# Reordered loads and split waits in the close of layer 0, early weights and a moved step in the scan of layer 1

## The chip, the core and the metric

The program runs on one core of a Trainium2 chip. The metric is the device time of one execution in microseconds (us). The engines are called PE (matmul, with PEld for its weight loads), DVE (vector), ACT (activations), POOL (GpSimd) and SP (the queue from which nearly all transfers of this kernel are issued). A matmul of float32 shows as two records.

## What is computed

The reference is two blocks of a network on 1024 tokens of width 1024. The first block has two layers; the second one (a hybrid mixer and 16 experts) is untouched here. What matters is the end of layer 0 and the start of layer 1:

```python
def _mixer_ab(...):                       # layer 0
    oa = dilated_attention(...)           # three dilations, merged by a softmax of their log sums
    ob = bidirectional_gated_scan(...)    # forward + backward, 4 heads of 256
    ob = _head_rmsnorm(ob, norm_gain)
    y = jnp.concatenate([oa, ob], axis=-1) * jax.nn.silu(gate)
    return jnp.einsum('bsf,fd->bsd', y, w_out)

def _mixer_c(...):                        # layer 1
    proj = jnp.einsum('bsd,df->bsf', h, w_in)
    q, f_f, f_b, i, gate = _split(proj, (C_WIDTH,) * 5)        # 12 heads of 128
    f = lb + (1.0 - lb) * jax.nn.sigmoid(z)                    # forward and backward
    o = bidirectional_gated_scan(silu(q) * s, 1 - f, log(f), ..., i)
    ...
x = _layer_norm(DEEPNORM_ALPHA * x + y, ln_gain[layer], ln_bias[layer])
```

## The kernel before

The program is a chain of stages. Each stage allocates its buffers and semaphores, runs one instruction stream per engine, and ends in a barrier of all engines. Two stages are touched.

**The close of layer 0** (`close_layer`, tag `end`, from 1061 to 1304 us) works on 8 tiles of 128 tokens. Below, n is the tile; the first two and the last two are written out, the four between run in a loop. For a tile

- SP's `load` fetches `of` and `ob` (the scan forward and backward, 512 KB each), `gt` (the gate, 768 KB) and `parts` (the three attention parts, 792 KB), in this order, after `y_done` of the tile before. All four raise the one semaphore `loaded[b]`, on which DVE, ACT and POOL wait for all of them. `load_x` fetches the residual `xt`.
- `front`: DVE merges the parts (L1475 to L1501) into `y[:, 0:A]`, with one Exp by ACT (L1380) in the middle. POOL adds `of + ob` (L1352). ACT takes Silu of the gate (L1381), squares the sum (L1386) and takes the root (L1389). DVE scales by root and gain into `y[:, A:W]` (L1510, `normed`), POOL multiplies all of `y` by the gate (L1355, `y_done`).
- PE turns `y` (L1430), ACT copies it (L1397), PE multiplies by the weights `w` (L1448, 48 records, banks `ps_z[0]` then `ps_z[1]`, `z_made`), then turns the tile before (L1438).
- DVE adds the residual and normalizes (L1526 to L1537, `centred`), POOL multiplies by gain and adds the bias (L1364, L1366, `x_done`), SP stores.

On each engine `front` of tile n + 1 stands ahead of the rest of tile n. At the start SP issues `load(0, 0)`, the vectors `gains`, `lng` and `lnb` (512 KB each, on one semaphore `vec_loaded`, for which DVE waits ahead of everything), `w` (6144 KB, one transfer), `load_x(0, 0)`, and then `load(0, 1)`, which waits for `y_done`.

**The scan of layer 1** (`projected_scan`, tag `hgrn`, 1304 to 2304 us) computes the projections as it goes. A unit of columns (`f`, `q`, `vg`, ...) takes seven sub-products of a Strassen scheme, called fills: SNAP1, PLAIN, SNAP21, SNAP22, JOIN22, JOIN21, LAST. The weights come through a ring of three slots. Four banks `ps_w` take the fills in turn; SNAP21 accumulates in the bank of SNAP1, after ACT has copied it (`moved`). DVE makes four sums of activations (L441 to L446, `x_made`) and POOL four sums of weights per unit (L758, L760, L765, L772, `s_made`); SNAP21 needs the second of DVE and the third of POOL. ACT's first instruction is the Sigmoid of the bounds (L1200), which waits for `diff_done`; DVE raises that after its four sums (L1088). ACT's copies of fills (`take`) stand behind it.

Four units are computed ahead of the first step. Then come 96 steps, 8 for each of 12 heads; step p of head h is g = 8h + p. In a step PE does `front` of step g + 1 (scores L899; transposes L907, which wait for `out_moved` to reach g, that is for `move_out(g - 1)`), `update(g)` (L916), `output(g)` (L929, L932) and the fills planned for it. DVE and ACT prepare head h + 1 along the way by `prepare(h + 1, p)`: DVE's `sums` at p = 2 and 3 (L988 to L999, `rel_done`), its `spans_of` at p = 3 and 4 (L1007 to L1017, `points_done`), behind each other in its queue. ACT's own order in a step is

```python
                if g:
                    move_out(g - 1)
                    takes(of_step[g - 1])
                if (g + 1) % TILES < CARRIED and g + 1 < STEPS:
                    move_keys((g + 1) // TILES, (g + 1) % TILES)
                if h + 1 < heads:
                    prepare(h + 1, p)
```

and its `exps` at p = 3 and 4 wait for `rel_done`, compute `qd` and `kd` (L1171, L1172), wait for `points_done`, and compute `end_decay` and `pair_decay` (L1174, L1175). Users of the decays are DVE's `scale_keys` from p = 6 on and POOL's `scale_queries` of the next head.

## Time and profile before

| what | us |
|---|---|
| time, median of 3 runs | 4135.04 (4132.1 to 4139.99) |
| time of the profiled execution | 4133.34 |
| its span, first to last instruction | 4131.6 |
| close of layer 0: stage, PE busy | 243.00, 193.73 |
| scan, ahead of the steps (1304 to 1433): PE busy | 129.00, 121.74 |
| scan, 96 steps (1433 to 2304): PE busy | 871.00, 817.96 |
| whole span: PE, DVE, ACT, POOL busy | 3580.3, 1779.0, 1076.0, 1171.5 |

The profile is that of one execution. The time of that execution is 1.7 us above its span. A row of the timeline gives start, duration, engine, line, operation and shapes, a count if rows were merged, and in brackets how long the engine had sat idle before it and what ended that. In a row of waits stand the total, the number of times and the longest.

### The profile page before, as it was taken

The numbers are of one execution on the slowest core, as the hardware profiler recorded it, in microseconds if no ns is written. First come the engines' busy times: TensorE is split into PE (matmuls) and PEld (weight loads), VectorE is DVE, ScalarE is ACT, GpSimd is POOL, SyncE is SP. The second block draws the span as 40 slices with busy tenths as digits, with TensorE's granted clock in tenths as the row PEclk, the third lists the DMA queues.
The fourth block names the chain that finished last, engine by engine and source line by source line (L and its number), as shares of the span: only waits on it lengthen the run. The fifth ranks groups of instructions, "written<-read, shape, count | busy, mean of one in ns | idle before, by whom it ended". The sixth has DMA issues, their size and how long they took to land. (4 is left out here: it accounts for less than half of the span.)

```text
span 4131.6 us, 46995 instructions
## 1 busy us (share of the span) xinstructions
PE 3580.3 (87%) x16369; PEld 2331.9 (56%) x16369; DVE 1779.0 (43%) x4038; ACT 1076.0 (26%) x2201; POOL 1171.5 (28%) x940
## 2 busy tenths in 40 slices
PE   8889998888697999999988598998975776949996
PEld 4645676667443675675646445655655775424442
DVE  0025552433353266566575353243477577240001
ACT  1023433432232233233233252221212212211111
POOL 0000000333243355456555354000303445211110
PEclk9999999899898999999999797999997888969998
DMA  3264532231432111121111533113224721446996
GB/s 114 77 169 146 164 113 85 70 99 47 191 143 87 53 54 45 53 61 48 56 48 39 221 133 108 38 44 117 92 93 131 255 98 58 159 171 234 315 325 229
DMA packets 408272, 494.01 MB, mean 120 GB/s; under 512 B 70498, under 2 KB 314490, under 8 KB 408051
## 3 DMA queue, kind: packets, MB, share of 16 engines
q1 hardware_dynamic: 379431, 457.42, 33.3%
q0 software_dynamic: 4608, 16.78, 1.6%
q10 hardware_dynamic: 24012, 16.97, 1.3%
q8 instruction: 126, 2.06, 0.2%
q14 instruction: 95, 0.78, 0.1%
HBM read 362.32 MB, written 128.77 MB: 119 GB/s over the span
## 5 line engine op out<-in xcount | busy, mean ns | idle before, releaser
L817 POOL TENSOR_TENSOR hgrn_queries<-hgrn_qd,hgrn_pair_decay 128x640 f32<-128x640 f32 x192 | 274.7, 1450 | 324.3 <-PE hgrn_ps_a L932 290.1
L867 PE MATMUL hgrn_ps_w<-xT,hgrn_ring 128*128 128x512 f32 x432 | 195.6, 599 | 8.9 <-DMA hgrn_ring<-in_w_in_c_dram 8.9
L395 PE MATMUL gla_bg_ps<-gla_bg_w,xT 128*128 128x256 f32 x768 | 196.6, 403 | 4.0 <-DMA gla_bg_w<-in_w_in_ab_dram 4.0
L395 PEld LDWEIGHTS gla_bg_ps<-gla_bg_w,xT 128*128 128x128 f32 x768 | 151.8, 203 | 37.7 <-issue 10.6
L1448 PE MATMUL end_ps_z<-end_w,end_yT 128*128 128x512 f32 x384 | 169.7, 602 | 1.6 <-ACT end_yT L1397 1.6
L2535 PE MATMUL end_ps_z<-end_w,end_yT 128*128 128x512 f32 x384 | 167.0, 595 | 0.8 <-ACT end_yT L2463 0.8
L391 PE MATMUL att_bg_ps<-xT,att_bg_w 128*128 128x512 f32 (+1 forms) x288 | 136.9, 615 | 13.3 <-POOL att_ident L1755 13.3
L867 PEld LDWEIGHTS hgrn_ps_w<-xT,hgrn_ring 128*128 128x128 f32 x432 | 81.4, 193 | 101.2 <-issue 91.6
L45 POOL MEMSET gla_ident<- 128x128 f32 x1 | 0.2, 205 | 484.5 <-POOLq L34 484.5
L1037 DVE TENSOR_TENSOR hgrn_k_end<-hgrn_kd,hgrn_end_decay 128x128 f32<-128x128 f32 x168 | 126.7, 793 | 8.9 <-issue 2.2
L872 PE MATMUL hgrn_ps_w<-hgrn_ring,xT 128*128 128x256 f32 x576 | 130.3, 382 | 0.0
L867 PE MATMUL hgrn_ps_w<-hgrn_xs,hgrn_wsum 128*128 128x512 f32 x288 | 128.2, 592 | 0.0
L2048 POOL TENSOR_TENSOR gla_queries<-gla_qd,gla_pair_decay 128x640 f32<-128x640 f32 x64 | 89.9, 1423 | 131.1 <-PE gla_ps_o L2111 91.5
L2891 PE MATMUL in_ps<-hT_cols,in_w 128*128 128x512 f32 x288 | 126.2, 592 | 0.0
L1448 PEld LDWEIGHTS end_ps_z<-end_w,end_yT 128*128 128x128 f32 x384 | 73.7, 194 | 92.6 <-issue 89.8
L4751 PE MATMUL exp_ps_d<-expw_wd,exp_hidT 128*128 128x512 f32 x256 | 114.1, 599 | 11.0 <-ACT exp_hidT L4698 11.0
L395 PE MATMUL att_bg_ps<-att_bg_w,xT 128*128 128x256 f32 x512 | 123.4, 387 | 0.0
L2535 PEld LDWEIGHTS end_ps_z<-end_w,end_yT 128*128 128x128 f32 x384 | 72.7, 191 | 89.6 <-issue 88.3
L1874 ACT ACTIVATE att_p_sb<-att_s_sb,att_shift 128x256 f32<-128x256 f32 (+1 forms) x192 | 88.8, 464 | 121.3 <-DVE att_shift L1833 121.2
L227 PE MATMUL in_ps<-xT,in_wbuf 128*128 128x512 f32 x256 | 112.8, 604 | 8.6 <-PEq L34 8.6
L872 PEld LDWEIGHTS hgrn_ps_w<-hgrn_ring,xT 128*128 128x128 f32 x576 | 109.3, 193 | 14.6 <-issue 0.5
L4733 PE MATMUL exp_ps_g<-expw_wg,exp_xT 128*128 128x512 f32 x256 | 115.6, 605 | 0.7 <-ACT exp_xT L4687 0.7
(643 smaller groups left out, 7663.9 us busy)
## 6 DMA issues: line engine op xcount, KB each, us to landing
expw_wg<-in_exp_w_gate_dram SPq DMA_DIRECT2D x16, 2048.0 KB, 9.5
expw_wu<-in_exp_w_up_dram SPq DMA_DIRECT2D x16, 2048.0 KB, 16.3
expw_wd<-in_exp_w_down_dram SPq DMA_DIRECT2D x16, 2048.0 KB, 21.8
att_w_ada<-in_ada_w_dram SPq DMA_DIRECT2D x24, 1024.0 KB, 6.3
hgrn_ring<-in_w_in_c_dram SPq DMA_DIRECT2D x18, 1024.0 KB, 5.3
end_gt<-gate_l SPq DMA_DIRECT2D x16, 768.0 KB, 7.9
hgrn_ring<-in_w_in_c_dram SPq DMA_DIRECT2D x24, 512.0 KB, 5.5
hgrn_o<-hgrn_o_stage SPq DMA_DIRECT2D x192, 64.0 KB, 1.6
```

Source lines behind the costliest of these rows:

```text
L227: last = pe.matmul(bank[0:job.rows, 0:job.span], w[:, k, b * job.rows:(b + 1) * job.rows], job.acts[:, k, s:s + job.span], start=(k == 0), ...
L391: last = pe.matmul(bank[0:job.rows, 0:job.span], w[:, k, b * job.rows:(b + 1) * job.rows], job.acts[:, k, s:s + job.span], start=(k == 0), ...
L395: last = pe.matmul(bank[0:job.rows, q * job.width:(q + 1) * job.width], job.acts[:, k, t * P:t * P + job.rows], w[:, k, 0:job.width], star ...
L817: pool.tensor_tensor(queries[:, d, s, :].rearrange("p (b a c) -> p b a c", b=POINTS, a=PC), q, f, ALU.mult).then_inc(queries_done, 1)
L867: last = pe.matmul(bank[:, :], a[:, k, :], x(k), start=(fresh and k == 0), stop=(k == HK - 1), skip_group_check=True)
L872: last = pe.matmul(bank[:, q * 2 * P:(q + 1) * 2 * P], x(k)[:, t * P:(t + 1) * P], a[:, k, :], start=(fresh and q == 0 and k == 0), stop=( ...
L1037: dve.tensor_tensor(k_end[:, d, p % 2, :].rearrange("p (a c) -> p a c", c=CH), kd[:, b, d, t * P:(t + 1) * P].rearrange("p (a c) -> p a c" ...
L1448: made = pe.matmul(ps_z[h][:, :], yT[:, k, :], w[:, k, h * BANK:(h + 1) * BANK], start=(k == 0), stop=(k == NB - 1))
L2535: made = pe.matmul(ps_z[h][:, :], yT[:, k, :], w[:, k, halves[h]], start=(k == 0), stop=(k == NB - 1))
L2891: last = pe.matmul(ps[(3 * n + part) % 2][:, 0:span], w[u % 3][:, k, b * P:(b + 1) * P], acts, start=(k == 0), stop=(k == KB - 1))
L4733: last = pe.matmul(ps_g[:, :], xT[:, b, k, :], wg[:, b, k, :], start=(k == 0), stop=(k == KB - 1))
L4751: last = pe.matmul(ps_d[g][:, :], hidT[:, j, :], wd[:, b, j, g * BANK:(g + 1) * BANK], start=(j == 0), stop=(j == FB - 1))
```

## The change

- `load` issues `parts` first, on a semaphore of its own (`parts_loaded`), then `of` and `ob` on `loaded`, then `gt` on `gt_loaded`. DVE waits for the parts alone, POOL for `of` and `ob`, ACT's Silu for the gate.
- DVE's wait for all three vectors goes. It waits for `gains` where L1510 first uses them; POOL waits for the other two ahead of its first slot.
- `w` comes in two halves of 512 columns, each with a semaphore; PE waits for a half ahead of the 24 records that use it, in the first tile.
- POOL multiplies `y` by the gate in two pieces: `y[:, 0:A]` once the merge is done, `y[:, A:W]` after `normed`.
- The ring of the scan is allocated around both stages. SP issues its first three blocks (3 MB in four transfers) in the last slot of the close, after the store of tile 6 and ahead of the wait for tile 7, and waits for them at the end of the stage. In the scan, waits for these blocks go.
- ACT's two decay factors leave `exps` and become `decays(h, d)`, both called at p = 5. Ahead of the steps the order stays.

```diff
+def scan_weights(sp, ring, w, C, loaded):
+    rows = w.rearrange("(k p) n -> p k n", p=P)
+    for slot, at, col, width in ((0, 0, C, P), (0, P, 2 * C, P), (1, 0, 0, 2 * P), (2, 0, 3 * C, 2 * P)):
+        sp.dma_start(ring[:, slot, :, at:at + width], rows[:, :, col:col + width]).then_inc(loaded, 16)
+    return 64
...
-        counts[slot_of(b)] += 16 * len(cols)
+        counts[slot_of(b)] += 16 * len(cols) if b >= RING else 0
...
-            load(0)
             sp.dma_start(bound_in[:, :, :], bounds.rearrange("(h p) c -> p h c", p=P)).then_inc(bounds_loaded, 16)
-            for b in range(1, RING):
-                load(b)
...
+            def decays(h, d):
                 act.wait_ge(points_done, 2 * h + d + 1)
                 act.activation(end_decay[:, h % 2, d, :], ends[:, d, :], ACT.Exp)
                 act.activation(pair_decay[:, h % 2, d, :], pairs[:, d, :], ACT.Exp).then_inc(decay_done, 1)
...
                 elif p in (3, 4):
                     exps(h, p - 3)
+                elif p == 5:
+                    decays(h, 0)
+                    decays(h, 1)
...
                 wait(sp, y_done, 2 * i + b)
+                if attn is not None:
+                    sp.dma_start(parts[:, :, :], attn[:, rows(i, b), :].rearrange("a p n -> p a n")).then_inc(parts_loaded[b], 16)
                 sp.dma_start(of[:, b, :], o[0][rows(i, b), :]).then_inc(loaded[b], 16)
                 sp.dma_start(ob[:, :], o[1][rows(i, b), :]).then_inc(loaded[b], 16)
-                sp.dma_start(gt[:, b, :], gate[rows(i, b), :]).then_inc(loaded[b], 16)
-                if attn is not None:
-                    sp.dma_start(parts[:, :, :], attn[:, rows(i, b), :].rearrange("a p n -> p a n")).then_inc(loaded[b], 16)
+                sp.dma_start(gt[:, b, :], gate[rows(i, b), :]).then_inc(gt_loaded[b], 16)
...
-            sp.dma_start(w[:, :, :], w_out.rearrange("(k p) n -> p k n", p=P)).then_inc(w_loaded, 16)
+            for h in range(2):
+                half = slice(h * BANK, (h + 1) * BANK)
+                sp.dma_start(w[:, :, half], w_out.rearrange("(k p) n -> p k n", p=P)[:, :, half]).then_inc(w_loaded[h], 16)
...
+                if last:
+                    ahead_due.append(ahead(sp, ahead_loaded))
                 sp.wait_ge(x_done, 2 * i + b + 1)
...
-                pool.wait_ge(loaded[b], 16 * LOADS * i + 16 * LOADS)
+                pool.wait_ge(loaded[b], 32 * i + 32)
                 pool.tensor_tensor(of[:, b, :], of[:, b, :], ob[:, :], ALU.add).then_inc(summed, 1)
+                pool.wait_ge(gated, n + 1)
+                if A:
+                    pool.wait_ge(merged_done, n + 1)
+                    pool.tensor_tensor(y[:, 0:A], y[:, 0:A], gt[:, b, 0:A], ALU.mult)
                 pool.wait_ge(normed, n + 1)
-                pool.wait_ge(gated, n + 1)
-                pool.tensor_tensor(y[:, :], y[:, :], gt[:, b, :], ALU.mult).then_inc(y_done, 1)
+                pool.tensor_tensor(y[:, A:W], y[:, A:W], gt[:, b, A:W], ALU.mult).then_inc(y_done, 1)
...
                 for h in range(2):
+                    if first:
+                        pe.wait_ge(w_loaded[h], 16)
...
-            dve.wait_ge(vec_loaded, 48)
             front(0, 0)
```

## Rows read from the trace of the kernel before

**Rows 1.** Busy time by engine in the scan's steps.

```profile
1433.00:2304.00 871.00, 817.96 (x4726) 546.53 (x4724) 534.00 (x1079) 277.42 (x466) 465.96 (x288) 0.97 0.17 52
```

**Rows 2.** Timeline of the close, tile 0.

```profile
1074.52 0.17 DVE L1475 TENSOR_TENSOR end_top<-end_parts 128x8 f32<-128x8 f32 x1 [23.11 <-DMA end_lnb<-in_ln_bias_dram]
...
1083.61 3.42 POOL L1355 TENSOR_TENSOR end_y<-end_y,end_gt 128x1536 f32<-128x1536 f32 x1 [11.25 <-DVE end_y L1510]
...
1090.71 0.50 PEld L1448 LDWEIGHTS end_ps_z<-end_w,end_yT 128*128 128x128 f32 x2 [1.15 <-DMA end_w<-in_w_out_ab_dram]
1090.74 23.62 PE L1448 MATMUL end_ps_z<-end_w,end_yT 128*128 128x512 f32 x48 [0.78 <-ACT end_yT L1397]
```

**Rows 3.** Transfers of 1061 to 1090 us: total; size and us to landing.

```profile
DMA packets 2923, 10.95 MB, mean 378 GB/s; under 512 B 128, under 2 KB 128, under 8 KB 2922
...
end_w<-in_w_out_ab_dram SPq DMA_DIRECT2D x1, 6144.0 KB, 25.9
```

**Rows 4.** Transfers of the close's inner tiles, 1120 to 1240 us.

```profile
end_parts<-attn SPq DMA_DIRECT2D x4, 792.0 KB, 8.3
...
end_of<-gla_o SPq DMA_DIRECT2D x4, 512.0 KB, 3.6
```

**Rows 5.** PE's timeline in the close, tiles 4 and 7.

```profile
1190.66 1.52 PE L1430 MATMUL end_ps_y<-end_ident,end_y 128*128 128x128 f32 x12 [1.53 <-POOL end_y L1355]
...
1192.98 20.87 PE L1448 MATMUL end_ps_z<-end_w,end_yT 128*128 128x512 f32 x48
...
1266.28 2.16 PE L1430 MATMUL end_ps_y<-end_ident,end_y 128*128 128x128 f32 x12 [3.11 <-POOL end_y L1355]
```

**Rows 6.** DVE and POOL in the close around tiles 4 and 5.

```profile
1200.57 2.34 POOL L1352 TENSOR_TENSOR end_of<-end_of,end_ob 128x1024 f32<-128x1024 f32 x1 [1.46 <-DMA end_parts<-attn]
...
1211.77 3.42 POOL L1355 TENSOR_TENSOR end_y<-end_y,end_gt 128x1536 f32<-128x1536 f32 x1 [8.87 <-DVE end_y L1510]
1219.11 2.35 POOL L1364 TENSOR_TENSOR end_xn<-end_z,end_lng 128x1024 f32<-128x1024 f32 x1 [3.91 <-DVE end_z L1537]
...
1200.64 2.29 DVE L1475 TENSOR_TENSOR end_top<-end_parts 128x8 f32<-128x8 f32 x1 [6.45 <-DMA end_parts<-attn]
```

**Rows 7.** Timeline of the scan's entry, by engine.

```profile
1311.26 8.88 PE L867 MATMUL hgrn_ps_w<-xT,hgrn_ring 128*128 128x512 f32 x16 [8.94 <-DMA hgrn_ring<-in_w_in_c_dram]
1319.98 7.03 PE L867 MATMUL hgrn_ps_w<-hgrn_xs,hgrn_wsum 128*128 128x512 f32 x16
...
1311.02 2.29 DVE L446 TENSOR_TENSOR hgrn_xs<-xT,hgrn_xs 128x2048 f32<-128x2048 f32 x1
...
1314.50 0.21 ACT L1200 ACTIVATE hgrn_low<-hgrn_room 128x12 f32<-128x12 f32 x1 [9.22 <-DVE hgrn_room L1088]
...
1311.29 3.15 POOL L758 TENSOR_TENSOR hgrn_wsum<-hgrn_ring 128x512 f32<-128x512 f32 x1 [10.98 <-DMA hgrn_ring<-in_w_in_c_dram]
```

**Rows 8.** Waits of PE and ACT in the scan's steps, 1433 to 2303 us.

```profile
ACT hgrn_end_decay L1174 <- DVE hgrn_pairs L1017: 55.0, 13, 5.8
...
PE hgrn_ps_a L907 <- ACT hgrn_o_stage L1186: 27.1, 8, 5.8
...
PE hgrn_ps_w L867 <- DVE hgrn_q_act L966: 13.3, 5, 2.7
```

**Rows 9.** Timeline of steps 3 and 4 of head 2, ACT and PE.

```profile
1639.75 1.04 ACT L1172 ACTIVATE hgrn_kd<-hgrn_cum 128x1024 f32<-128x1024 f32 x1
1644.73 0.24 ACT L1174 ACTIVATE hgrn_end_decay<-hgrn_ends 128x40 f32<-128x40 f32 x1 [3.94 <-DVE hgrn_pairs L1017]
...
1634.05 0.44 PE L907 MATMUL hgrn_ps_a<-hgrn_ident,hgrn_k_end 128*128 128x128 f32 x2
...
1635.67 7.07 PE L872 MATMUL hgrn_ps_w<-hgrn_wsum,hgrn_xs 128*128 128x256 f32 x32
...
1645.61 0.41 PE L907 MATMUL hgrn_ps_a<-hgrn_ident,hgrn_k_end 128*128 128x128 f32 x2 [2.44 <-ACT hgrn_o_stage L1186]
...
1648.37 4.09 PE L872 MATMUL hgrn_ps_w<-hgrn_ring,xT 128*128 128x256 f32 x16
```

More of the change, by code:

```diff
@@ L446, in strassen_sums, with projected_scan @@
     dve.tensor_tensor(xs[:, 2, :, :], x(1, 0), xs[:, 1, :, :], ALU.subtract).then_inc(made, 1)
-def projected_scan(nc, tag, heads, xT, w, bounds, out, gate_out, spill, q_scale):
+def scan_weights(sp, ring, w, C, loaded):
[3 more added lines that the diff above has]
+    return 64
+def projected_scan(nc, tag, heads, xT, w, ring, bounds, out, gate_out, spill, q_scale):
     PC = P // CH
@@ L581, in projected_scan @@
         pbank = lambda n: ctx.enter_context(nc.psum_tensor(f"{tag}_{n}", [P, BANK], F32))
-        ring = sb("ring", [P, RING, KB, 2 * P])
         xs = sb("xs", [P, 3, HK, BANK])
@@ L754, in sums_early @@
                 for n in range(1 if narrow(units[u][0][0]) else 2):
-                    pool.wait_ge(w_loaded[slot_of(b + n)], loads_by[b + n])
+                    wait(pool, w_loaded[slot_of(b + n)], loads_by[b + n])
                 if u:
@@ L851, in fill @@
                     for m in range(1 if narrow(kind) else 2):
-                        pe.wait_ge(w_loaded[slot_of(b + m)], loads_by[b + m])
+                        wait(pe, w_loaded[slot_of(b + m)], loads_by[b + m])
                 e = before_on[f]
@@ L1205, in _ @@
             exps(0, 0)
+            decays(0, 0)
             takes(lead[18:25])
             exps(0, 1)
+            decays(0, 1)
             takes(lead[25:])
@@ L1228, in row_to_all, with close_layer @@
     return vector.rearrange("(a n) -> a n", a=1).to_broadcast([P, n])
-def close_layer(nc, tag, x, x_next, xT_next, o, gate, gain, w_out, ln_gain, ln_bias, V, alpha, attn=None, attn_heads=0):
+def close_layer(nc, tag, x, x_next, xT_next, o, gate, gain, w_out, ln_gain, ln_bias, V, alpha, ahead, attn=None, attn_heads=0):
     WO = o[0].shape[1]
@@ L1272, in close_layer @@
         ps_x = [pbank(f"ps_x{n}") for n in range(2)]
-        vec_loaded, w_loaded, consts = sem("vec_loaded"), sem("w_loaded"), sem("consts")
-        LOADS = 3 if attn is None else 4
+        vec_loaded, w_loaded, consts = sem("vec_loaded"), [sem("w_loaded0"), sem("w_loaded1")], sem("consts")
         loaded = [sem("loaded0"), sem("loaded1")]
+        gt_loaded, parts_loaded = [sem("gt_loaded0"), sem("gt_loaded1")], [sem("parts_loaded0"), sem("parts_loaded1")]
         x_loaded = [sem("x_loaded0"), sem("x_loaded1")]
+        gains_loaded, merged_done = sem("gains_loaded"), sem("merged_done")
         summed, squared, gated = sem("summed"), sem("squared"), sem("gated")
@@ L1323, in _ @@
             load(0, 0)
-            for dst, src in ((gains, gain), (lng, ln_gain), (lnb, ln_bias)):
+            sp.dma_start(gains[:, :], row_to_all(gain, WO)).then_inc(gains_loaded, 16)
+            for dst, src in ((lng, ln_gain), (lnb, ln_bias)):
                 sp.dma_start(dst[:, :], row_to_all(src, dst.shape[1])).then_inc(vec_loaded, 16)
-            sp.dma_start(w[:, :, :], w_out.rearrange("(k p) n -> p k n", p=P)).then_inc(w_loaded, 16)
+            for h in range(2):
+                half = slice(h * BANK, (h + 1) * BANK)
+                sp.dma_start(w[:, :, half], w_out.rearrange("(k p) n -> p k n", p=P)[:, :, half]).then_inc(w_loaded[h], 16)
             load_x(0, 0)
@@ L1500, in front @@
                         if a:
-                            dve.tensor_tensor(y[:, 0:A], y[:, 0:A], merged[:, :], ALU.add)
+                            last = dve.tensor_tensor(y[:, 0:A], y[:, 0:A], merged[:, :], ALU.add)
                             dve.drain()
+                    last.then_inc(merged_done, 1)
                 dve.wait_ge(squared, n + 1)
@@ L1507, in front @@
                 dve.drain()
+                if isinstance(i, int) and n == 0:
+                    dve.wait_ge(gains_loaded, 16)
                 for h in range(H):
@@ L4806, in network @@
             ])
-        close_layer(nc, "end0", x[0], x1, xT, gla_o, gate_l0, gla_norm[0], w_out_ab[0], ln_gain[0], ln_bias[0],
-                    B // 4, alpha, attn=attn, attn_heads=AH)
-        gate_l1 = dram("gate_l1", SEQ, C)
-        hgrn_o = [dram(f"hgrn_o{d}", SEQ, C) for d in range(2)]
-        projected_scan(nc, "hgrn", C // P, xT, w_in_c[0], hgrn_bounds, hgrn_o, gate_l1, dram("v_spill", SEQ, 2 * P), scale)
+        with nc.sbuf_tensor("hgrn_ring", [P, 3, KB, 2 * P], F32) as ring:
+            close_layer(nc, "end0", x[0], x1, xT, gla_o, gate_l0, gla_norm[0], w_out_ab[0], ln_gain[0], ln_bias[0],
+                        B // 4, alpha, lambda sp, loaded: scan_weights(sp, ring, w_in_c[0], C, loaded), attn=attn, attn_heads=AH)
+            gate_l1 = dram("gate_l1", SEQ, C)
+            hgrn_o = [dram(f"hgrn_o{d}", SEQ, C) for d in range(2)]
+            projected_scan(nc, "hgrn", C // P, xT, w_in_c[0], ring, hgrn_bounds, hgrn_o, gate_l1, dram("v_spill", SEQ, 2 * P), scale)
     poolT = dram("poolT", 2 * P, SEQ)
```

10 lines of the change are left out of this document (6 added, 4 removed).

## The prediction, on record before the change was run

> **What bounds the kernel now.** I read the windows by stage first. In the steps of the scan PE is busy 818 of 871 us [rows 1], so nearly every us there is PE's, and only what holds PE up can be won. Then the timeline of the close, for what each tile waits for; then the transfers; then the waits of PE in the scan, and around one of them the timelines of ACT and PE. The stages are divided by barriers, so what a stage gains the end of the program gains, unless a later stage waits for something else.
>
> The first tile of the close is a chain. DVE starts at 1074.5 because of the last of three vectors, not because of its data; POOL finishes `y` at 1087.0, and PE multiplies from 1090.7 [rows 2]. The queue moves 10.95 MB in this time at 378 GB/s, and `w` lands 25.9 us after its issue at 1064.4, so at 1090.3 [rows 3]: chain and weights end together. In the inner tiles PE waits some 1.5 us per tile for POOL's `y`, and 3.1 us at tile 7 [rows 5]; such a tile takes 1215.33 - 1190.66 = 24.7 us, and 23.2 without its wait. At the scan's entry PE waits for the ring until 1311.3 [rows 7]. In the steps PE waits 8 times, 27.1 us, for ACT's `move_out`, which stands behind ACT's own wait for `spans_of` [rows 8].
>
> **Part 1, the close.** *Start.* With parts first and no vector ahead of DVE, the merge starts when the parts land. `of`, as first transfer, lands after 3.6 us; parts, as fourth, after 8.3 [rows 4]. Scaled by size, parts as first take some 4.5 us, so they land at 1065.5, and DVE starts 9 us earlier. But the same bytes come before the gate: the four transfers (2.6 MB) have landed by about 1070, one table load and Silu, squares, root and scaling (8.3 us from there) follow, then the last two thirds of POOL's 3.42 us [rows 2]: `y` is done at about 1080.7 instead of 1087.0. The multiplication starts 3.4 us later as before, at 1084.1, 6.6 us earlier. It needs only the first half of `w`. Of the 10.5 MB up to the end of `w` the first half needs 7.4; with `w` whole at 1090.3 and 3.15 MB at some 390 GB/s [rows 3] it is there at about 1082.3. The second half is needed 12 us after the start; covered. If rows of 2 KB run a tenth slower than those of 4 KB, `w` is whole 1.6 us later, and the first half comes at 1083; still covered, but the next tile's loads queue behind it.
>
> *Tile 1.* Its loads queue behind `w` as before, until about 1091.7, so its gate lands no earlier than before (about 1099); only the order gains: `y` at about 1109.7 instead of 1114.6. PE, ready at 1107.7, waits 2 us. The multiplication starts at 1112.5 instead of 1117.0: 4.5 us are left of the 6.6.
>
> *Inner tiles.* Let T be `z_made`. The multiplication began at 1192.98 and took 20.87 us [rows 5], so T = 1213.85, and DVE has centred the tile when POOL's L1364 starts, at T + 5.3 [rows 6]. Until now DVE then waited for data; now the parts are there, and it starts at once. From L1475 to L1355 the front took 1211.77 - 1200.64 = 11.1 us, of which 2.1 in a lock: a DVE operation on 128x8 elements took 2.29 us beside POOL's L1352 [rows 6]. The new start puts DVE under three POOL operations (L1364, L1366, L1352), not one, so two more locks of 2.35: T + 5.3 + 11.1 + 4.7 = T + 21.1, then POOL's second piece (2.3) and about 0.9 in which the first piece holds DVE: T + 24.3. PE alone gives 23.2 per tile, and `y` of tile n + 2 hangs on T of tile n: two tiles in 23.2 + 24.3 = 47.5, or 23.2 to 23.75 a tile. I take 23.4, against 24.7: 1.3 for each of tiles 3 to 6. Tile 2 started its multiplication 27.4 us after tile 1, because of 2.6 us of wait and a low clock; it gains 4. Tile 7 gains 2.5 of 3.1 and the lower clock behind. Sum: 4.5 + 4 + 4 x 1.2 + 2 = 15. Bounds: 8 if the locks eat all gain of the inner tiles, 18 if none costs.
>
> Here the Trainium skill says the same of the cause ("SBUF — State Buffer", Who interferes with whom, and SBUF: two separate sides): DVE with two SBUF inputs and a GpSimd operation exclude each other for the whole instruction. By that rule every POOL operation that now lies over the merge costs its full length; without the lock the loop would be PE's alone, 23.2 a tile, and this part 18. The row agrees: 2.29 us for 8 elements.
>
> **Part 2, the ring at the scan's entry.** The four transfers are issued after the store of tile 6 and land within some 10 us, 20 us ahead of the barrier; they delay only the issue of the last store's wait, covered. PE can start at the entry, R = 1304, not 1311.3. What is late next: SNAP21, at R + 16.0 before [rows 7]. It needs ACT's copy of SNAP1, and ACT's queue begins with L1200, which waits for DVE's four sums. Before, these ran alone (L446, the last, from 1311.02 to 1313.31), L1200 ran at R + 10.5, and POOL's first sum took 3.15 us, because it waited for the end of L446; its own time is what is left, 1.1 to 1.27 [rows 7]. Now POOL's four sums start with DVE's four. Taking turns they end at R + 9.3 + 4 x 1.2 = R + 14.1; L1200, the copy (0.6) and three handoffs end at R + 15.2. PE gains 0.8 us. But its idle time now lies behind its first 16 records, not ahead: after 8.94 us idle they took 8.88 us instead of 7.03 [rows 7], and after 6.3 us idle I charge the same 1.85 again. Sum: 1.0 us lost. Bounds: 1.9 lost (clock alone) to 4.4 won (no lock, SNAP21 at R + 11.6, clock kept). The records on either side decide for the lock, so I take 1 lost.
>
> **Part 3, the decays.** The step of [rows 9]: ACT finishes `kd` at 1640.8 and could do `move_out` then, but waits for `spans_of` until 1644.7; PE's transposes, due at 1643.2, start at 1645.6. From transposes to fill PE took 2.76 us, against 1.62 in the step before, and 16 records of the fill 3.92 against 3.45: the clock had dropped. So 2.4 + 1.1 + 0.5 = 4.0 us a time. With the decays at p = 5, `move_out` is done at 1641.2, before PE is due. This pattern comes in heads 0, 2, 4, 6: 16 us. The other four waits (17.2 of the 27.1 us) are in heads 8 and 10, which have few fills. There PE, once free at p = 3, meets ACT held at p = 4 by the wait that stays, for `sums` (L999), which itself sits under POOL's operations. I follow both: about 3 us each are left. In the odd heads PE waits for DVE's join (13.3 us, 5 times [rows 8]); the change does not touch it. The decays cost 0.24 and 0.32 us, at p = 5 in odd heads with one more table load; ACT is busy 277 of 871 us [rows 1], and `move_out(5)` behind them has a whole step before PE needs it. Sum 22; bounds 14 (if half of the waits come back as waits for L999) and 27 (the waits in full, nothing behind).
>
> **Sum**, against the profiled execution's 4133.3: -15 + 1 - 22 = -36, so 4097.3; the median of the runs stood 1.7 above that execution: 4099.
>
> **Rivals.**
> - *The decay waits move* to L999 in all heads, or to `pick`, which stands behind `spans_of` in DVE's queue. For: DVE has no gap in this stretch. Against: in heads 0 to 6 L999 is done before PE is due. Then part 3 gives 10 to 12: 4110. Chance 0.2.
> - *The lock eats the close's loop*: tiles stay at 24.7, part 1 gives 8: 4106. Chance 0.12.
> - *The ring gives its whole wait*: no turns taken, SNAP21 at R + 11.6, clock kept: part 2 wins 4.4: 4094, and to 4091 with part 1 at its bound. Speaks against it the 3.15 us row. Chance 0.1.
> - *The change does not do what it says*: waits as before: 4133. Chance 0.03.
> - *Slower*: the decays at p = 5 come late for their users at p = 6 and the next head's queries. Then each of 11 heads waits; with the gains of the close it decides from (36 + 8) / 11 = 4 us per head on. Against: a step is about 9 us long and the decays need 1.1. Price at 5 us per head: 4144. Chance 0.05.
> - The forecast itself: 0.5.
>
> 0.2% (8 us) is what a measurement of this kernel can tell from no change. Faster by more: 0.9; within: 0.06; slower: 0.04. The bounds of the parts together are -53 and -20; all at one end is unlikely, and the rivals reach 4110: range 4084 to 4115.
>
> **What would show it.** Right: DVE's first merge near 1065.5; `y` of tile 0 near 1080.7; multiplications starting 23.2 to 23.8 apart; DVE's 128x8 operations of 2 us under L1364 and L1366; PE's first record in the scan at the entry, then a gap of 5 to 7 us ahead of the second group of 16; no waits of L907 for L1186 in heads 0 to 6, some of 3 to 4 us in heads 8 and 10. Wrong: a loop at 24.7; SNAP21 11 to 12 us behind the entry; transposes waiting for ACT in every even head.

## The result

The changed kernel takes 4102.4 us (median of 4 runs, 4101.2 to 4110.4), the kernel before 4134.1 (4 runs): a ratio of 0.9924, 95% interval 0.9911 to 0.9936, so 31.7 us less. The forecast was 4099. The profiled execution has a span of 4101.0 us at a mean clock of 0.924.

The windows first: the steps of the scan in the changed kernel, the stretch that answers to [rows 1].

```profile
1416.00:2267.00 851.00, 810.48 (x4727) 540.63 (x4725) 539.37 (x1079) 283.81 (x471) 469.11 (x288) 0.98 0.18 53
```

The same number of matmuls to one record (4727, 4726 before), in 851 us instead of 871. PE is idle for 41 us instead of 53, and has 7.5 us less of busy time, which is the clock (the granted clock is 0.98, not 0.97). Now the timeline of the close, tile 0, against [rows 2]:

```profile
1065.61 0.17 DVE L1498 TENSOR_TENSOR end_top<-end_parts 128x8 f32<-128x8 f32 x1 [14.13 <-DMA end_parts<-attn]
1066.76 1.28 ACT L1404 ACT_TABLE_LOAD   x1
1070.07 1.48 ACT L1404 ACTIVATE end_gt<-end_gt 128x1536 f32<-128x1536 f32 x1 [2.03 <-DMA end_gt<-gate_l]
...
1077.13 2.34 POOL L1377 TENSOR_TENSOR end_y<-end_y,end_gt 128x1024 f32<-128x1024 f32 x1 [1.55 <-DVE end_y L1536]
...
1083.37 20.84 PE L1473 MATMUL end_ps_z<-end_w,end_yT 128*128 128x512 f32 x48 [0.96 <-DMA end_w<-in_w_out_ab_dram]
1109.79 2.82 PE L1453 MATMUL end_ps_y<-end_ident,end_y 128*128 128x128 f32 x12 [5.58 <-POOL end_y L1377]
```

The reader is to see DVE's start 8.9 us earlier, `y` at 1079.5 (1080.7 was forecast), the first half of `w` landing just as PE wants it, and 5.6 us of PE's wait for tile 1's `y`. DVE and POOL around tile 5, against [rows 6]:

```profile
1187.69 1.45 DVE L1498 TENSOR_TENSOR end_top<-end_parts 128x8 f32<-128x8 f32 x1 [1.00 <-DMA end_parts<-attn]
...
1189.45 4.48 DVE L1503 TENSOR_TENSOR end_lift<-end_parts,end_top 128x8 f32<-128x8 f32 x3
...
1191.56 2.35 POOL L1371 TENSOR_TENSOR end_of<-end_of,end_ob 128x1024 f32<-128x1024 f32 x1
...
1202.62 2.34 POOL L1377 TENSOR_TENSOR end_y<-end_y,end_gt 128x1024 f32<-128x1024 f32 x1 [1.55 <-DVE end_y L1536]
...
1205.10 1.52 PE L1453 MATMUL end_ps_y<-end_ident,end_y 128*128 128x128 f32 x12
1206.46 1.04 PE L1461 MATMUL end_ps_x<-end_ident,end_xn 128*128 128x128 f32 x8
1207.41 20.87 PE L1473 MATMUL end_ps_z<-end_w,end_yT 128*128 128x512 f32 x48
```

`y` is done at 1204.96, and PE turns it at 1205.10 with no wait. The eight multiplications start at 1083.37, 1113.30, 1138.03, 1161.35, 1184.32, 1207.41, 1230.43 and 1253.40, the inner ones 23.0 to 23.3 apart. The scan's entry, against [rows 7], PE and then ACT:

```profile
1287.41 8.87 PE L871 MATMUL hgrn_ps_w<-xT,hgrn_ring 128*128 128x512 f32 x16 [1.77 <-PEq L34]
1301.57 8.63 PE L871 MATMUL hgrn_ps_w<-hgrn_xs,hgrn_wsum 128*128 128x512 f32 x16 [5.29 <-ACT hgrn_sig L1153]
...
1300.82 0.21 ACT L1209 ACTIVATE hgrn_low<-hgrn_room 128x12 f32<-128x12 f32 x1 [12.17 <-DVE hgrn_room L1092]
1300.94 0.58 ACT L1153 ACTIVATE hgrn_sig<-hgrn_ps_w 128x512 f32<-128x512 f32 x1
```

PE starts at the entry, then stands for 5.3 us, and its second group is 14.2 us behind the entry where it was 15.9 (14.8 and 15.1 in two more profiles with the old entry, before_again and only_decays). The waits of PE in the steps, against [rows 8]:

```profile
PE hgrn_ps_s L903 <- DVE hgrn_state L1071: 16.4, 3, 10.7
PE hgrn_ps_w L871 <- DVE hgrn_q_act L970: 13.2, 5, 2.7
PE hgrn_ps_s L903 <- POOL hgrn_queries L821: 5.5, 3, 2.7
```

The 27.1 us for ACT's `move_out` are gone but for 0.3. The second row was there before. The first is all but new (0.6 us before): 10.7 us of it are one wait in head 8. In head 2, 0.8 us of wait for DVE's `k_end` took the place of the old one.

### The profile page after: what moved, and what is told of

Read it like the earlier page. It is cut to its first block and busy times, and to the rows that moved or that the text cites. A ratio compares the mean times of both kernels' runs of the same rounds, so it can differ in the third digit from the quotient of the medians.

```text
span 4101.0 us, 47003 instructions
## 1 busy us (share of the span) xinstructions
PE 3579.0 (87%) x16369; PEld 2330.3 (57%) x16369; DVE 1812.7 (44%) x4038; ACT 1081.5 (26%) x2206; POOL 1183.6 (29%) x948
## 5 line engine op out<-in xcount | busy, mean ns | idle before, releaser
L876 PE MATMUL hgrn_ps_w<-hgrn_ring,xT 128*128 128x256 f32 x576 | 128.8, 380 | 0.0
L876 PEld LDWEIGHTS hgrn_ps_w<-hgrn_ring,xT 128*128 128x128 f32 x576 | 108.0, 191 | 14.2 <-issue 0.5
## 6 DMA issues: line engine op xcount, KB each, us to landing
expw_wg<-in_exp_w_gate_dram SPq DMA_DIRECT2D x16, 2048.0 KB, 10.3
```

What stands on the lines that cost most here:

```text
L876: last = pe.matmul(bank[:, q * 2 * P:(q + 1) * 2 * P], x(k)[:, t * P:(t + 1) * P], a[:, k, :], start=(fresh and q == 0 and k == 0), stop=( ...
```

## Where the time went, stage by stage

Four marks cut each profile: the scan's entry (DVE's first sum), the start of PE's third group of 16 fill records there, PE's first record of the next layer's close, and PE's first record in the experts' stage. The columns are the entry's time from the span's start, and then the three stretches, in us. All kernels of the study are in it, those of the next section too.

```
kernel               entry     to group 3   to next close   to experts
before               1304.04   22.81        1002.05         1393.87
before_again         1302.42   21.69        1001.74         1393.79
only_decays          1301.54   21.94         981.92         1400.75
after                1287.41   22.63         981.76         1400.84
after_again          1286.29   22.66         981.67         1403.45
no_ring              1284.95   22.20         984.24         1399.01
w_whole              1288.17   23.71         982.76         1401.42
parts_last           1285.55   24.07         983.22         1409.85
one_piece            1287.95   24.04         983.29         1403.43
copy_first           1286.93   15.65         984.70         1398.44
no_ring_copy_first   1284.28   22.19         982.26         1400.43
spans_later          1287.48   22.83         965.18         1401.25
both                 1284.69   15.67         965.12         1400.00
after_delayed        1287.20   22.64        1015.68         1400.35
```

The first profile against the first: 16.6 us won up to the entry, 0.2 at the entry, 20.3 in the scan's steps, and 7.0 lost in stages that the change does not touch; 30.1, of a difference of spans of 30.6. The same kernel repeats to 0.1 or 0.3 us in the steps, but the old close ended at 1301.5, 1302.4 and 1304.0 in three profiles, so the first one flatters the change: against their mean 15.8 were won up to the entry (two profiles of the changed kernel: 1286.9), and the entry lost 0.5 (22.65 against 22.15). That 0.5 lies within the spread of the old entry, 21.7 to 22.8, so whether the entry lost or won a little is not shown.

The column of the entry also holds the stages ahead of the close, which no edit touches: the close issues its first load between 1058.6 and 1061.9 us in the fourteen profiles. Measured from that issue, the close took 243.0, 240.5 and 240.3 us before (before, before_again, only_decays), and 226.3 and 226.2 in the changed kernel: 15.0 us won against the mean. In w_whole it took 227.6, in parts_last and one_piece 226.9. One profile with the changed close stands apart, no_ring_copy_first with 222.6; its second multiplication started 1.9 us and its third 3.6 us sooner behind the first load than in the changed kernel.

The profiles overstate what was given back behind. The two profiled executions of the kernel before took 4133.3 and 4128.3 us, both below the median of its 34 runs in the whole study (4135.3). By the medians 31.7 us were won.

## The experiments

**only_decays.** The kernel before with the decays in a step of their own, nothing else.

```diff
                 act.activation(kd[:, h % 2, d, :], ...)
+
+            def decays(h, d):
                 act.wait_ge(points_done, 2 * h + d + 1)
...
+                elif p == 5:
+                    decays(h, 0)
+                    decays(h, 1)
```

> The kernel before with one part of the change alone: the decays at p = 5. Theory (the parts add up): in the steps of the scan it gains what the changed kernel gained there, 20.3 us between the third group of the entry and the first multiplication of the next close; the eight waits of L907 for ACT's move_out are gone, in heads 8 and 10 PE waits for DVE's state instead, 10 and 5 us. Close and entry as before. Time: 20 us less at the start of the next close, and 15 to 20 less at the end, by whether the stages behind give something back. Rival (part of the 20 us came from the close, by a better clock or another phase at the start): under 15 us in the steps.

4117.7 us, 0.9966 of the kernel before (0.9954 to 0.9978), 14 us less by the ratio, 16 by the medians of the two. The steps took 981.92 us: 20.0 less, as in the changed kernel. The parts add up, and some of the 20 us are missing at the end here too: 7 by the last column (1400.75), 4 to 6 by the times. Its waits in the steps:

```profile
PE hgrn_ps_s L899 <- DVE hgrn_state L1067: 16.8, 2, 11.3
PE hgrn_ps_w L867 <- DVE hgrn_q_act L966: 13.3, 5, 2.7
```

So the new wait comes with the decays, not with the close or the ring.

**no_ring.** The changed kernel, its ring loaded at the scan's entry as before.

```diff
-                if last:
-                    ahead_due.append(ahead(sp, ahead_loaded))
...
+            load(0)
             sp.dma_start(bound_in[:, :, :], ...)
+            for b in range(1, RING):
+                load(b)
```

> The changed kernel without its ring ahead: the four transfers at the scan's entry, as before. Theory (PE's second group is set by ACT's queue, whose first entry waits for DVE's four sums): PE starts 7.3 us behind the entry, the second group of 16 at about 16.0 us, the third at 22.9; the changed kernel had the third at 22.65, so this one is within 1 us of it. Rival (the early ring is worth its wait): 5 to 7 us slower than the changed kernel.

4101.7 us (0.9928, 0.9915 to 0.9942), against 4102.4: the early ring is worth nothing. The second group followed the first without a gap and at full clock (granted clock 1.00, 0.82 in the changed kernel's second group), and the third started 22.20 us behind the entry:

```profile
1291.20 9.24 PE L874 MATMUL hgrn_ps_w<-xT,hgrn_ring 128*128 128x512 f32 x16 [8.03 <-DMA hgrn_ring<-in_w_in_c_dram]
1300.28 7.03 PE L874 MATMUL hgrn_ps_w<-hgrn_xs,hgrn_wsum 128*128 128x512 f32 x16
```

**copy_first.** The changed kernel; ACT copies the first group's bank before its Sigmoid of the bounds.

```diff
+            lead = of_step[-1]
+            takes(lead[0:1])
             act.wait_ge(diff_done, 1)
             act.activation(low[:, :], room[:, :], ACT.Sigmoid).then_inc(low_done, 1)
-            lead = of_step[-1]
-            takes(lead[0:7])
+            takes(lead[1:7])
```

> The changed kernel with one step of ACT's queue put ahead: the copy of the first group's bank (L1153) before the Sigmoid of the bounds (L1209), which waits for DVE's four sums. Theory (the order in ACT's queue holds SNAP21): the copy runs at about 5.5 us behind the entry, POOL's third sum is done at 7.8, so the second group follows the first at 8.9 without a gap, at full clock (7.0 us, not 8.6), and the third starts at 16 to 17 instead of 22.65: 5.5 to 7 us less at the first step. Rival A (the turns that DVE and POOL take set it): second group at 13 to 14, gain under 1 us. Rival B (the next wait, DVE's first join behind the same Sigmoid, takes it over): 1 to 4 us of gain are left.

4093.2 us (0.9901, 0.9886 to 0.9917), 9 us less than the changed kernel, by intervals that just overlap; the stages tell more. The entry, POOL, ACT and PE:

```profile
1291.61 3.11 POOL L769 TENSOR_TENSOR hgrn_wsum<-hgrn_ring 128x512 f32<-128x512 f32 x1 [0.16 <-issue]
1292.48 0.60 ACT L1153 ACTIVATE hgrn_sig<-hgrn_ps_w 128x512 f32<-128x512 f32 x1 [6.69 <-PE hgrn_ps_w L871]
...
1295.71 7.03 PE L871 MATMUL hgrn_ps_w<-hgrn_xs,hgrn_wsum 128*128 128x512 f32 x16
...
1302.58 3.60 PE L871 MATMUL hgrn_ps_w<-xT,hgrn_ring 128*128 128x512 f32 x8
```

The copy ran 5.6 us behind the entry, the second group 8.8 behind it, and the third 15.65: 7.0 us sooner. DVE and POOL still took turns (3.11 us for a sum that alone takes 1.26), and it did not matter. The order of ACT's queue was what held SNAP21; at the entry both rivals fell. Not all of the 7.0 reached the next close: the steps took 984.70 us, 2.9 more than in the changed kernel. One fill, behind PE's wait for DVE's join in head 3, took 6.78 us here and 3.70 there. In both (below), where that wait is short, nothing is lost.

**no_ring_copy_first.** Both edits above.

> The kernel with the copy ahead, without the early ring. Theory (the ring ahead is worth its time only when ACT's queue does not hold SNAP21): PE starts 6 us behind the entry, its second group follows without a gap at about 15, the third at 22: 5.5 us later than with the early ring and about as without either edit, so 5 to 6 us slower than the kernel with both. Rival (the ring ahead is worth nothing in any order): same as that kernel within 1 us.

4104.3 us (0.9926, 0.9912 to 0.9939), 10 to 11 us slower than with the early ring, again by intervals that overlap a little. The third group started at 22.19, to 0.01 where no_ring had it: without the early ring the copy's place is worth nothing, without the copy's place the ring is worth nothing, together they are worth 7 at this point.

**spans_later.** The changed kernel; DVE prepares the points of the first direction one step later.

```diff
                 elif p == 3:
-                    spans_of(h, 0)
                     sums(h, 1)
                 elif p == 4:
+                    spans_of(h, 0)
                     spans_of(h, 1)
```

> The changed kernel with DVE's spans_of for the first direction moved from p = 3 to p = 4, beside that for the second. Theory (in heads 8 and 10 PE waits for the state, L1071, which stands in DVE's queue behind spans_of and sums, 11.2 us at one stretch, 5 of them spans_of): the waits of 10.7 and 5.1 us shrink to 4 to 6 and 0 to 2, and since p = 4 then holds both spans_of, up to half comes back there: 3 to 8 us less in the steps of the scan, all in these two heads. Rival (DVE is the bound in these two heads whatever the order): the sum of the waits stays at 16, the time too.

4083.2 us (0.9878, 0.9863 to 0.9893), 19 us less than the changed kernel, 16.6 of them in the steps: my theory was wrong in size and in place. The waits in the steps:

```profile
PE hgrn_ps_s L903 <- POOL hgrn_queries L821: 13.9, 4, 8.4
PE hgrn_ps_s L903 <- DVE hgrn_state L1071: 6.6, 4, 2.8
PE hgrn_ps_w L871 <- DVE hgrn_q_act L970: 3.6, 5, 0.7
```

In heads 8 and 10 the wait for the state only changed its name: 16.4 + 5.5 us for state and queries became 6.6 + 13.9. There the rival was right, DVE and POOL are the bound. The gain came from the odd heads' wait for DVE's join, which fell from 2.65 to 0.71 us, five times (9.7 us):

```profile
1538.51 3.70 PE L871 MATMUL hgrn_ps_w<-xT,hgrn_wsum 128*128 128x512 f32 x8 [0.71 <-DVE hgrn_q_act L970]
```

Behind the short wait the fill takes 3.70 us (granted clock 1.00). Behind the long one it had taken 5.4 in four of the five places (granted clock 0.68), and that is nearly all of the rest. From one such wait to the next, two heads on, it is 153.4 us; in the changed kernel it was 155.3 to 157.9. DVE's queue in p = 3 had held the join all along.

**both.** copy_first and spans_later together.

> The two edits that gained, together in the changed kernel: ACT's copy of the first group's bank ahead of its Sigmoid of the bounds, and spans_of of the first direction at p = 4. Theory (they act in different stretches and add up): the third group of the entry 7.0 us earlier, the steps from there to the next close 16.6 us shorter, so about 23 to 26 us less than the changed kernel: 4076 to 4080. Rival (what is won is given back in the stages behind): under 17 us.

4076.0 us (0.9859, 0.9843 to 0.9875), 26 us less than the changed kernel and 58 to 61 less than the one before. The table has 15.67 at the entry and 965.12 in the steps: each edit's full gain.

**w_whole.** The changed kernel with `w` in one transfer.

```diff
-            for h in range(2):
-                half = slice(h * BANK, (h + 1) * BANK)
-                sp.dma_start(w[:, :, half], ...).then_inc(w_loaded[h], 16)
+            sp.dma_start(w[:, :, :], ...).then_inc(w_loaded[0], 16)
```

> The changed kernel with w in one transfer again, PE waiting for all of it. In the changed kernel the first multiplication started at 1083.37, when w's first half had landed, ended about 1104, and PE then waited 5.6 us for y of tile 1. Theory (tile 1's y sets the loop's start, whose data lie behind w in the queue; the halves win time that tile 1 gives back): the first multiplication starts 6 to 7 us later, at about 1090, PE's wait for y of tile 1 goes to nothing, the second one starts at 1113.5 to 1115, so 0 to 2 us are lost. Rival (the first tile's 7 us count in full): 6 us lost. The prediction's own bookkeeping (1112.5 against 1117.0) had the first half's 6.6 us worth 4.5.

4105.6 us (0.9922, 0.9909 to 0.9936), the same as the changed kernel. The first multiplication started 6.5 us later, the second 2.5 and the third 0.8:

```profile
1089.90 23.83 PE L1471 MATMUL end_ps_z<-end_w,end_yT 128*128 128x512 f32 x48 [8.11 <-DMA end_w<-in_w_out_ab_dram]
1113.57 1.47 PE L1451 MATMUL end_ps_y<-end_ident,end_y 128*128 128x128 f32 x12
1115.83 20.87 PE L1471 MATMUL end_ps_z<-end_w,end_yT 128*128 128x512 f32 x48 [0.79 <-ACT end_yT L1418]
```

In the changed kernel PE waited 5.6 us for tile 1's `y`, and its second multiplication took 22.63 us (granted clock 0.92); here there is no such wait, and it takes 20.87 (1.00). The close is 1.3 us longer (227.6): the halves are worth about 1 us.

**parts_last.** The changed kernel, the attention's parts fourth again in each tile's loads.

```diff
-                if attn is not None:
-                    sp.dma_start(parts[:, :, :], ...).then_inc(parts_loaded[b], 16)
                 sp.dma_start(of[:, b, :], ...)
                 sp.dma_start(ob[:, :], ...)
                 sp.dma_start(gt[:, b, :], ...)
+                if attn is not None:
+                    sp.dma_start(parts[:, :, :], ...).then_inc(parts_loaded[b], 16)
```

> The changed kernel with the attention's parts fourth again in each tile's loads, behind both halves and the gate. Theory (the order of the loads is what shortens the inner tiles: DVE no longer waits for data): DVE's merge starts 3 to 5 us later in each tile, y comes that much later, the inner tiles go back from 23.2 to 24.5 to 25 us, and the close is 8 to 12 us longer than in the changed kernel. Rival (the pieces of POOL's multiplication and the late waits carry the gain, the order does not): within 3 us of the changed kernel.

The theory fell. From the third on the multiplications are 23.0 and 23.5 to 24.0 apart in turns (117.1 us from the third to the last, 115.4 in the changed kernel), and the close as a whole takes 226.9 us, 0.6 more than in the changed kernel. Tile 5 again, DVE and POOL:

```profile
1188.58 2.34 POOL L1371 TENSOR_TENSOR end_of<-end_of,end_ob 128x1024 f32<-128x1024 f32 x1
1189.31 1.64 DVE L1498 TENSOR_TENSOR end_top<-end_parts 128x8 f32<-128x8 f32 x1 [5.59 <-DMA end_parts<-attn]
1191.27 0.32 DVE L1503 TENSOR_TENSOR end_lift<-end_parts,end_top 128x8 f32<-128x8 f32 x3
...
1200.26 2.34 POOL L1377 TENSOR_TENSOR end_y<-end_y,end_gt 128x1024 f32<-128x1024 f32 x1 [1.55 <-DVE end_y L1536]
```

DVE starts 4.6 us later behind the end of the multiplication two tiles back (10.1 us, not 5.5), but POOL's three operations are all but over by then: L1503 takes 0.32 us and not 4.48. `y` comes 23.35 us behind that end, against 22.7. The whole program took 4109.9 us (0.9934, 0.992 to 0.9949), 4 us more than the changed kernel by the ratio and 7.5 by the medians. The table has them in its last column, not in the close. Most of them can be placed: the stage of the second block with the tag `gdns` took 136.5 us here and 129.6 in the changed kernel. DVE there, in parts_last and then in the changed kernel, and POOL in parts_last:

```profile
3245.50 6.74 DVE L4089 TENSOR_TENSOR gdns_resid<-gdns_vb,gdns_rest 128x384 f32<-128x384 f32 x1
...
3242.36 2.02 DVE L4089 TENSOR_TENSOR gdns_resid<-gdns_vb,gdns_rest 128x384 f32<-128x384 f32 x2
...
3245.50 1.61 POOL L3978 TENSOR_TENSOR gdns_kw<-gdn_k_n,to_end 128x384 f32<-128x384 f32 x2
3247.07 1.61 POOL L3997 TENSOR_TENSOR gdns_kept<-gdns_state,gdns_col 128x384 f32<-128x384 f32 x2
```

One DVE operation took 6.74 us, where two take 2.02. It started together with a row of eight POOL operations, one behind the other, and ended 0.4 us after the last of them; PE's next product stood for 7.5 us. In none of the other thirteen profiles does a DVE operation of this stage take over 2.2 us. Whether the other executions of parts_last have it too is not known.

**one_piece.** The changed kernel, POOL's multiplication by the gate undivided.

```diff
                 pool.wait_ge(gated, n + 1)
-                if A:
-                    pool.wait_ge(merged_done, n + 1)
-                    pool.tensor_tensor(y[:, 0:A], y[:, 0:A], gt[:, b, 0:A], ALU.mult)
                 pool.wait_ge(normed, n + 1)
-                pool.tensor_tensor(y[:, A:W], y[:, A:W], gt[:, b, A:W], ALU.mult).then_inc(y_done, 1)
+                pool.tensor_tensor(y[:, :], y[:, :], gt[:, b, :], ALU.mult).then_inc(y_done, 1)
```

> The changed kernel with POOL's multiplication by the gate undivided again (one operation of 3.4 us behind DVE's last, not 1.2 under DVE and 2.3 behind it). Theory (y of tile n + 2 hangs on the multiplication of tile n, as the prediction had it, and in the changed kernel y comes just as PE is free, at 23.0 to 23.3 a tile): y comes 1.1 us later, two tiles take 23.2 + 24.3 instead of 23.2 + 23.2, so 0.5 us a tile and 2 to 4 us in the close. Rival (DVE's own work without POOL's first piece beside it ends earlier, 0.9 us, and PE's slack covers the rest): under 1 us.

4102.8 us (0.9918, 0.9903 to 0.9934). In the close: `y` 23.4 us behind the end of the multiplication two tiles back, PE waits 0.8, 0.56 and 0.31 us for it in every second tile, and the last multiplication starts at 1253.92, 0.5 us later than in the changed kernel. The model of two tiles in 23 + 23.4 held: 117.3 us from the third multiplication to the last, not 115.4, so 1.9 lost there. Tile 1 gives most of it back: PE waits 2.6 us for its `y`, not 5.6, and the second multiplication takes 20.87 us, not 22.63. The close is 0.6 us longer in all (226.9).

**before_again, after_again, after_delayed.** The two kernels profiled once more (one execution each, 4128.3 and 4103.6 us), and the changed kernel with 32 unused copies of 128x1024 elements on ACT at the scan's end (one execution, 4134.8 us).

> The kernel before, profiled once more. The stages behind the next close took 1393.9 us from its first multiplication to the first of the experts in the profile of before, and 1398.4 to 1401.3 in five profiles of changed kernels, whose code there is the same. Theory (these 5 to 7 us are when the clock comes back up, which differs between executions, and the profiled one of before had it early): this time 1398 to 1401. Rival (it depends on the kernel, because a shift of the start shifts the clock's steps against the work): 1394 again.

> The changed kernel profiled once more, for the spread of a stage between executions: from the first multiplication of the next close to the first of the experts it took 1400.8 us in its first profile, 1393.9 and 1393.8 in the two of the kernel before, whose code there is the same. If it is chance, this one may lie anywhere from 1394 to 1401; if it goes with the kernel, at 1400 to 1401.

> The changed kernel with work put in that uses nothing: at the end of the scan's stage ACT copies 128x1024 elements 32 times, some 35 us, so that the stages behind start at about the time at which they start in the kernel before (multiplication of the next close at 2325 to 2330). Theory A (what the stages behind gave back goes with the time at which they start, through the clock's steps): from there to the experts 1394 us, as in the kernel before. Theory B (it does not go with the start): 1398 to 1401, as in the eight other profiles of changed kernels.

The last column of the table gave 1393.8 again for the kernel before, 1403.5 for the changed one, and 1400.4 for the delayed one, whose next close started at 2325.5, as in before_again. So what is given back does not go with the time of the start, and two profiles against twelve speak against chance alone. Part of it lies in the stage `gdns`: it took 126.1 and 126.3 us in the two profiles of before, 128.3 to 131.7 in eleven of changed kernels, and 136.5 in parts_last. The windows of its first 30 us and of the rest, before, before_again and then after and after_delayed:

```profile
3254.83:3284.83 30.00, 19.58 (x118) 18.65 (x119) 10.79 (x19) 4.73 (x5) 20.64 (x23) 0.68 0.87 312
3284.83:3380.87 96.04, 76.96 (x640) 75.20 (x639) 65.12 (x133) 12.82 (x26) 41.50 (x53) 0.89 0.47 162
```

```profile
3251.96:3281.96 30.00, 19.28 (x116) 18.35 (x117) 10.62 (x19) 4.72 (x5) 20.42 (x23) 0.68 0.87 317
3281.96:3378.22 96.26, 77.33 (x642) 75.57 (x641) 65.31 (x133) 12.80 (x26) 41.69 (x53) 0.89 0.47 160
```

```profile
3221.02:3251.02 30.00, 20.31 (x96) 19.67 (x97) 8.59 (x14) 4.72 (x5) 20.06 (x23) 0.56 0.84 305
3251.02:3350.58 99.56, 81.03 (x662) 79.27 (x661) 66.95 (x137) 12.80 (x26) 42.16 (x53) 0.88 0.47 159
```

```profile
3255.97:3285.97 30.00, 19.72 (x109) 18.82 (x110) 10.04 (x17) 4.72 (x5) 21.11 (x24) 0.64 0.90 321
3285.97:3386.32 100.35, 81.26 (x650) 79.75 (x648) 66.19 (x134) 12.80 (x26) 40.99 (x52) 0.85 0.45 153
```

The granted clock (the column before the last two) of the first 30 us is 0.68 in both profiles of before, 0.56 and 0.64 in the others, and the 758 or 759 matmul records of the stage keep PE busy 96.5 and 96.6 us in the first two, 101 in the others. But w_whole has 128.8 us for the stage with PE busy for 96.9, so the clock is not the whole of it. Of the rest, the close behind the scan has up to 1.7 us (225.4 and 225.6 us before, 225.7 to 227.2 in the others).

## Why the prediction was right, and where it was not

In short: the total came out, 4102.4 against 4099, and part of that is luck. Within the close the terms missed both ways and cancelled, the cause of the inner tiles' gain was read wrongly, and the decays were charged too much.

*Start of the close.* Right, nearly term by term: DVE at 1065.6 (1065.5; the "Scaled by size" behind it gives 5.6 us for the parts, not 4.5, so this hit was partly luck), `y` at 1079.5 (1080.7), the multiplication at 1083.4 (1084.1). The 1.2 us of `y` came from ACT's table load, which I had put behind the gate's landing; it ran before it. `w`'s first half was forecast for 1082.3 to 1083, "still covered". It landed at 1083.2 (issued at 1064.7, 18.5 us), just behind the end of ACT's last copy of `y` at 1083.04, and so it set the start, by some 0.2 us at most: the rest of PE's wait of 0.96 us is for that copy (0.78 us before).

*Tile 1.* `y` at 1109.75 (1109.7), the multiplication at 1113.3 (1112.5). I had charged PE 2 us of wait; it was 5.6, since the first multiplication ran at full clock, 20.8 us. "4.5 us are left" became 3.7, and w_whole shows how little the first tile matters: its multiplication started 7.0 us later behind the close's first load, and the close was 1.3 us longer.

*Inner tiles.* 23.1 each (23.4 forecast). The locks came, somewhat smaller than charged: L1498 and L1503 took 5.9 us, of which 1.45 + 4.48 - 0.17 - 0.32 = 5.4 was lock, against 2.1 from before and 4.7 more, 6.8, in the forecast. `y` came at T + 22.7, not T + 24.3, and PE's own time bounded the loop. The Trainium skill ("SBUF — State Buffer", Who interferes with whom, and SBUF: two separate sides) has the loser block for the whole of the other's instruction; parts_last is the counterpart, the same three operations in 0.32 us with POOL idle. What I read wrongly is the gain's cause. I had "the parts are there, and it starts at once"; yet from the third multiplication to the last the old close took 125.6, 123.3 and 123.1 us in its three profiles, the new one 115.4, and with the parts fourth, or POOL's piece undone, it is 117.1 and 117.3. Either way `y` comes 23.4 us behind T instead of 26.1 (T = 1189.13, `y` at 1215.19), and DVE's early start is paid back in locks. What all three kernels share is that each engine waits for its own transfer; that this alone would do was not run, so it is argued, not shown. The sum, 15, was measured as 15.0 from the close's first load, against three profiles of the old close. Its terms were not: up to tile 1 3.8 us (4.5), tile 2 2.5 (4, since the low clock stayed in tile 1's multiplication), tiles 3 to 6 5.1 (4.8), tile 7 3.5 (2).

*The ring.* Right in that it gave nothing: 1.0 us lost forecast, 0.5 measured, 0.2 won against the first profile; the spread of the old entry, 1.1 us, is wider than both. The reasons held. SNAP21 came at 14.2 us (15.2), behind ACT's copy, its Sigmoid, and DVE's four locked sums; its 16 records took 8.63 us, 1.6 more (1.85 forecast), at a granted clock of 0.82. copy_first and no_ring_copy_first show the cause; the forecast's upper bound, 4.4 us won, was still short of what the order of one queue was hiding, 7.

*The decays.* 20.2 us instead of 22. The four waits for ACT in heads 0, 2, 4 and 6 are gone. The step that failed is "4.0 us a time": I measured one stall, in head 2, with its clock loss, and multiplied by four. From fill to fill the heads gained 2.5, 4.1, 3.9 and 2.5 us in only_decays, 13.0 in all against 16: two of the four cost only their 2.45 us of wait. (In the changed kernel they gained 2.5, 3.3, 3.9 and 2.5, and the fill behind the join in head 3 another 1.7, at full clock there alone.) Heads 8 and 10 gave 3.6 and 3.4 in only_decays (3 each forecast), but PE did not meet ACT at p = 4, it met DVE's queue: the state's update behind `spans_of` and `sums`, 11.1 us in one piece, DVE and then PE:

```profile
2067.81 2.35 DVE L1011 TENSOR_TENSOR hgrn_points<-hgrn_totals,hgrn_to_mid 128x32 f32<-128x32 f32 x1
...
2077.66 1.23 DVE L1003 TENSOR_TENSOR hgrn_cum<-hgrn_cum,hgrn_mids 128x1024 f32<-128x1024 f32 x1
2079.75 0.61 DVE L1071 SCALAR_TENSOR_TENSOR hgrn_state<-hgrn_state,hgrn_end_decay,hgrn_ps_s 128x128 f32<-128x128 f32 x2 [0.16 <-issue]
...
2080.50 0.77 PE L903 MATMUL hgrn_ps_s<-hgrn_queries,hgrn_kd 128*32 128x128 f32 x16 [10.71 <-DVE hgrn_state L1071]
```

And the odd heads' join wait, which I left standing as untouched, was the largest thing still to be had: one call one step later took 16.6 us from it and the clock behind it.

*The sum.* -15.0 + 0.5 - 20.2 = -34.7 in the three parts, against -36. What failed besides is the sentence "what a stage gains the end of the program gains, unless a later stage waits for something else". No later stage waited, and yet they took 1398 to 1410 us in twelve profiles of changed kernels and 1393.8 in both of before. By the medians 3.0 of the 34.7 us are missing at the end (31.7 were won); the profiles, whose two executions of the old kernel lie below its median, say 7 to 10. The distance from 4099 to 4102.4 is these 3.0 us, and 1.3 by which the parts fell short, less 0.9 by which the old kernel's median (4134.1) lay under the 4135.0 of the forecast. The stage `gdns` has 2.1 to 5.6 us of what the profiles say (10.3 in parts_last), mostly at a lower granted clock. Why it goes with the kernel, in a stage whose code is the same, stays open: a delay that restored the start did not bring the higher clock back, and only_decays, one edit on ACT, had the loss already. parts_last's last column, 6 to 8 us above its neighbours, is mostly the one long DVE operation shown above; why it happened in that execution is open.

## What to carry to other kernels

An early transfer is worth what the next thing behind it allows: list what the second instruction waits for, in which queue, and what stands ahead of it there. Here a ring loaded 7 us early gave nothing until a copy was put ahead of a Sigmoid, and then gave the 7.

When one wait for many loads is split, and orders are changed at the same time, undo them one by one before crediting one: gains that PE's own time caps do not add up, and each looks sufficient alone.

A stall's price includes the clock behind it, and that differs from one stall to the next of the same pattern: 2.45 us of wait cost 2.5 in two heads and 3.9 to 4.1 in two others (only_decays). Read each before multiplying. And what a stage wins is not what the program wins until the stages behind it have been laid side by side. Measure a stage from its own first instruction, too: here the stages ahead shifted its end by up to 3 us.

## What the hardware showed that was not expected

- At the scan's entry DVE and POOL, with a stream each of two-input operations, took strict turns: in the changed kernel POOL's 128x512 sums took 1.26, 3.11, 3.12 and 3.11 us, DVE's 128x2048 sums 3.40, 3.17, 3.35 and 3.17 instead of 2.29. Neither ran two in a row. The turns cost DVE 3.9 us over four, and POOL 5.6 over three. It is not always so: in parts_last one DVE operation that takes about 1 us otherwise took 6.74, while eight POOL operations ran in a row.
- ACT's table load did not wait for the data of the activation that it served: it ran at 1066.76 for 1.28 us, and the activation at 1070.07 when its gate had landed, so the load cost nothing there. In the kernel before, where ACT's program has two waits in a row ahead of its Exp, the load of tile 5 ran at 1200.59, once the first of them had ended.
- The stages behind the change, to the instruction the same, took 5 to 16 us longer in all twelve profiles of changed kernels than in both profiles of the old one. By the medians of the runs the loss is smaller, about 3 us for the changed kernel.
